# Keys as seven block products beside the values, sums of weight blocks in planes and in two stages

## The chip, the cores and the metric

The kernel runs on one core of a Trainium2 chip. The metric is the device time in microseconds of one execution; lower is better. The engines are TensorE (PE, its weight loads PEld), VectorE (DVE), ScalarE (ACT), GpSimd (POOL) and SyncE (SP), which issues nearly all DMAs.

## The reference

A trunk of two layers for 512 tokens of 2048 channels, in float32. What matters here is in the middle: after layer A, shared keys and values are projected from the residual stream, and layer B attends over them.

```python
kv = _rmsnorm(x, kv_norm) @ w_kv                      # 2048 x 4096: keys, then values
k = kv[..., :D_ATTN].reshape(bsz, s, N_HEADS, HEAD_DIM)   # 16 heads of 128
v = kv[..., D_ATTN:].reshape(bsz, s, N_HEADS, HEAD_DIM)
...
h = _rmsnorm(x, b_norm[lb])
proj = h @ b_w_in[lb]                                 # queries, then gates
o = _stick_breaking_attention(q, k, v)                # z = q k^T, sigmoids, a reverse running product, @ v
x = x + (o * jax.nn.silu(gate)) @ b_w_out[lb]
return _rmsnorm(x, final_norm)
```

## The kernel before, in words

Every float32 operand is split in two float32r parts, high and low, and a product is three matmuls: high by high, high by low, low by high (`product`, L730, whose matmul is at L733). ScalarE makes the high part of a staged weight tile (L1069 and L1071 with a gain for each row tile, L1067 without, L1209 and L1211 for the block products), VectorE the low part (L1538, L1540, L1535, L1748, L1751). A semaphore counts each step, and a tile of weights runs through a ring of four buffers: SyncE loads it when the low part of the tile four before is made, ScalarE splits it when TensorE has used the one four before.

There are five stages.

1. Layer A: 180 units of input projection and gates. A *unit* (`unit_t`, L737) is 256 rows by 256 columns of weights, weights still and all 512 tokens moving: 12 matmuls of 512 columns. Beside it, sums of 2 x 2 blocks of the value weights are made by VectorE (`block_sum`, L1685) from blocks that SyncE loads (`blocks_in`, L538) and stored to a scratch in HBM (`sums_out`, L548).
2. Output projection of layer A: 80 units. The new residual `x1` comes out in tiles of channels by tokens. GpSimd adds up token halves and channel pairs of it in `s_raw` (`token_sums`), the sums S1 to S4 of a Winograd form with seven products.
3. Values: `value_product` (L860). Seven block products p1 to p7 replace eight. VG = 2 groups of 1024 value columns, each of 7 x 8 = 56 products; a *block product* keeps 128 tokens still (twice) and moves 512 columns of weights: 6 matmuls of 512 columns. The operands come through six buffers (VRING), loaded in `operand_load` (L608). The results are drained and combined by ScalarE and VectorE into `v_f`, scaled by token and stored to a scratch (`v_store`, L598).
4. Layer B, in 8 pairs of heads: `pair_rest` (L959). N3 = 24 units each: 8 for queries, 8 for keys, 8 for gates (`src3`, L509). Its attention stands between units: scores of head 0 before unit 18, its transposes before unit 22, then, counted on into the next pair, scores of head 1 before unit 24 and so on to 30. `work3` (L1356 on ScalarE, L1918 on VectorE) gives the companions at the same positions. Queries are drained after unit 8 of a pair and keys after unit 16 (`kf`, L1929), both high parts are copied by ScalarE (L1361), both low parts subtracted by GpSimd (L2199), each in turn through the one tile `kf`. Sums of blocks of `b_w_out` are made beside it (`weight_sum`, `wb_load`, `wb_store`).
5. Output projection of layer B, again as block products (`out_product`), interleaved with the attention of the last pair, and the last norm.

VectorE's order within a pair is written out by hand in `body3` (L2051): the low part of unit q + 12, then a block sum if `W_SUM` names q, then `work3` for position q + 8. After the second head of a pair, that is `kf<-ps,sg` (L1884), three sums (L1899 to L1902), the next low part, two more sums (L1907, L1909). SyncE's order is written out in `weights3` (L661).

Of the kernel before, what the change touches and what calls it, by code (L numbers as in the profile page):

```python
# [27 lines left out]
F32 = mybir.dt.float32  # L28
# [5 lines left out]
P = 128  # L34
S = 512
# [20 lines left out]
N1, N2, N3 = 36, 20, 24  # L56
# [25 lines left out]
V_STORE, V_LOAD = 9, 18  # L82
# [10 lines left out]
VG, VP = 2, KD // 2  # L93
NO = 7 * VP
VOPS = VG * NO
VRING, AHEAD_V = 6, 5
# [11 lines left out]
T_IN, T_OUT = (16, 22, 34, 40), (27, 35, 45, 53)  # L108
T_SUM = {4: (0,), 5: (1,), 6: (2,), 7: (3,), 10: (4,), 11: (5,), 13: (6,), 16: (7, 8), 17: (9,)}
# [14 lines left out]

OPERAND = {operand(q): q for q in range(VOPS)}
OUT_LAST = 3


def out_operand(q):
# [9 lines left out]
    if g == VG - 1 and o >= 4 * VP:  # L139
        return g, (o - 4 * VP) % VP, ("p2", "p4", "p3")[(o - 4 * VP) // VP]  # L140
    return operand(q)


OUT_OPERAND = {out_operand(q): q for q in range(VOPS)}
OUT_RING = VOPS - VP
# [11 lines left out]
def build(nc, x, a_norm, a_w_in, a_conv_w, a_conv_b, a_w_r, a_b_r, a_w_i, a_b_i, a_lambda, a_w_out,  # L157
          kv_norm, w_kv, b_norm, b_w_in, b_w_out, final_norm, out):
    with ExitStack() as ctx:
# [56 lines left out]
        with ExitStack() as mem12:  # L216
# [13 lines left out]
            with ExitStack() as mem_v:  # L230
                v_f = sb("v_f", [P, TT, 1024], F32, mem_v)
# [3 lines left out]
                v_stage = sb("v_stage", [P, VRING - RING, 512], F32, mem_v)  # L235
        u2 = x1
        b_raw = b_raw0, b_raw1
        with ExitStack() as mem34:
# [11 lines left out]
            with ExitStack() as mem3:  # L250
                q_hi = sb("q_hi", [P, 2, S], F32R, mem3)
                q_lo = sb("q_lo", [P, 2, S], F32R, mem3)
# [74 lines left out]
        qk_f = sem("qk_f")  # L327
        qk_hi_ready = sem("qk_hi_ready")
        qk_lo_ready = sem("qk_lo_ready")
# [38 lines left out]
        wb_in = [sem(f"wb_in{n}") for n in range(2)]  # L368
# [31 lines left out]
        scaled_c = sem("scaled_c")  # L400
# [5 lines left out]
        def gain_column(phase, j):  # L406
# [3 lines left out]
            if phase == 3:  # L410
                return (C_GKV if j // 8 % 3 == 1 else C_GB) + 2 * (j % 8)
            return None

        def bank3(half, j):

            return 2 * ((3 * half + j // 8) % 2)
# [14 lines left out]
        def v_staged(q):  # L431

            slot = q % VRING
            return stage[:, slot, :] if slot < RING else v_stage[:, slot - RING, :]

        def v_weights(q):

            slot = q % VRING
# [3 lines left out]
        def kv_gain(k):  # L442

            return cT[:, C_GKV + k:C_GKV + k + 1]

# [33 lines left out]
        wt_scratch = nc.dram_tensor("wt_scratch", (4, VP * P, VG * 512), F32).ap()  # L479
        t_scratch = nc.dram_tensor("t_scratch", (4, VP * P, VG * 512), F32).ap()  # L480
# [6 lines left out]
        def _(sp):  # L487
# [1746 lines left out]
```

## Time and profile before

| | us |
|---|---|
| median of 3 runs (lowest, highest) | 1653.1 (1652.7, 1653.92) |
| profiled execution, whole | 1653.25 |
| its span in the profile | 1651.5 |
| TensorE busy | 1639.7 |
| VectorE busy | 1132.9 |
| ScalarE busy | 866.2 |
| GpSimd busy | 223.9 |
| mean DMA rate | 170 GB/s |

Busy times are sums over the span. Matmuls overlap their neighbours, so TensorE's busy share says that it is never idle for long, and not how fast it works: for that, the starts of successive matmuls are read. The stages in the trace: layer A to 506 us, its output projection to 731, the values to 887, the eight pairs to 1484, and the rest.

### The profile page before, as it was taken

What the parts mean: (1) busy time and instruction counts of PE and PEld (TensorE: products, weight loads), DVE (VectorE), ACT (ScalarE), POOL (GpSimd) and SP (SyncE); (2) the same over time, 40 slices, a digit from 0 to 9 for tenths busy, and PEclk for the clock granted to TensorE, in tenths of its full rate; (3) what the DMA queues carried; (4) which work ended last, traced back from release to release, by engine and by line L of the source; (5) the groups of instructions that cost most, each with busy time, mean ns of one, the idle gap of its engine ahead of it and who ended that gap; (6) DMA issues with size and microseconds to landing.
All of it is one profiled execution on the core that took longest, in us unless ns stands there. A gap on an engine that the chain in (4) does not pass through costs nothing.

```text
span 1651.5 us, 24337 instructions
## 1 busy us (share of the span) xinstructions
PE 1639.7 (99%) x7479; PEld 1364.7 (83%) x7479; DVE 1132.9 (69%) x1981; ACT 866.2 (52%) x1710; POOL 223.9 (14%) x221
## 2 busy tenths in 40 slices
PE   9999999999999999999999999999999999999997
PEld 8888888888888888888888888888888888888886
DVE  5788877778774545458654666666757576668867
ACT  7655566655565333346655544453545444446555
POOL 0121212121211313121000101110110101110000
PEclk9999999999999999999999999999999999999999
DMA  5556555655433343347675545445353636458875
GB/s 188 178 179 199 169 155 188 201 189 185 150 95 97 102 126 104 121 127 221 202 229 177 179 131 172 156 139 188 130 192 108 194 110 188 143 179 287 290 240 193
DMA packets 216839, 280.81 MB, mean 170 GB/s; under 512 B 16488, under 2 KB 145720, under 8 KB 216760
## 3 DMA queue, kind: packets, MB, share of 16 engines
q1 hardware_dynamic: 212152, 270.05, 51.4%
q10 hardware_dynamic: 4608, 9.83, 1.8%
q8 instruction: 34, 0.56, 0.1%
q14 instruction: 45, 0.37, 0.1%
HBM read 229.09 MB, written 50.72 MB: 169 GB/s over the span
## 4 chain that ended last, share of the span: by engine, by line
PE 96%; DVE 1%; ACT 1%; issue 0%; DMA 0%; POOL 0%; POOLq 0%; ACTq 0%; DVEq 0%
PE ps L733 94%; PE ps L943 1%; PE ps L763 0%; PE ps L833 0%; PE ps L789 0%; DVE oa_lo L1968 0%; DMA v_stage<-in_w_kv 0%; ACT rb L1460 0%; DVE x L2020 0%; ACT x L1506 0%; DVE rbuf L1677 0%; POOL y_lo L2133 0%; ACT w_hi L1067 0%; PE ps L770 0%; ACT abuf L1153 0%
## 5 line engine op out<-in xcount | busy, mean ns | idle before, releaser
L733 PE MATMUL ps<-x_hi,w_hi 128*128 128x512 f32 x1408 | 551.0, 391 | 0.1
L733 PE MATMUL ps<-x_hi,w_lo 128*128 128x512 f32 x1408 | 548.4, 389 | 0.0
L733 PE MATMUL ps<-x_lo,w_hi 128*128 128x512 f32 x1408 | 548.1, 389 | 0.0
L1538 DVE SCALAR_TENSOR_TENSOR w_lo<-stage,cT,w_hi 128x256 fp32r<-128x256 f32 x352 | 191.2, 543 | 285.1 <-ACT w_hi L1071 283.7
L1069 ACT ACTIVATE w_hi<-stage,cT 128x256 fp32r<-128x256 f32 x352 | 178.7, 508 | 374.7 <-PE ps L733 352.5
L733 PEld LDWEIGHTS ps<-x_hi,w_lo 128*128 128x128 f32 x1408 | 264.3, 188 | 55.0
L733 PEld LDWEIGHTS ps<-x_hi,w_hi 128*128 128x128 f32 x1408 | 264.5, 188 | 53.9 <-issue 0.7
L733 PEld LDWEIGHTS ps<-x_lo,w_hi 128*128 128x128 f32 x1408 | 264.5, 188 | 53.6 <-issue 0.2
L1071 ACT ACTIVATE w_hi<-stage,cT 128x256 fp32r<-128x256 f32 x352 | 174.4, 495 | 0.0
L1540 DVE SCALAR_TENSOR_TENSOR w_lo<-stage,cT,w_hi 128x256 fp32r<-128x256 f32 x352 | 172.4, 490 | 0.0
L1535 DVE TENSOR_TENSOR w_lo<-stage,w_hi 128x512 fp32r<-128x512 f32 x100 | 86.3, 864 | 116.5 <-ACT w_hi L1067 116.5
L1067 ACT ACTIVATE w_hi<-stage 128x512 fp32r<-128x512 f32 x100 | 62.6, 629 | 138.8 <-PE ps L733 138.1
L733 PE MATMUL ps<-y_hi,w_hi 128*128 128x512 f32 x320 | 125.3, 391 | 0.7 <-POOL y_lo L2133 0.7
L733 PE MATMUL ps<-y_hi,w_lo 128*128 128x512 f32 x320 | 124.6, 389 | 0.0
L733 PE MATMUL ps<-y_lo,w_hi 128*128 128x512 f32 x320 | 124.5, 389 | 0.0
L733 PEld LDWEIGHTS ps<-y_hi,w_hi 128*128 128x128 f32 x320 | 60.1, 188 | 13.2 <-POOL y_lo L2133 1.1
L733 PEld LDWEIGHTS ps<-y_hi,w_lo 128*128 128x128 f32 x320 | 60.1, 188 | 12.5
L733 PEld LDWEIGHTS ps<-y_lo,w_hi 128*128 128x128 f32 x320 | 60.1, 188 | 12.3
L1392 ACT ACTIVATE w_hi<-stage 128x512 fp32r<-128x512 f32 x70 | 43.8, 632 | 37.9 <-PE ps L733 34.7
L1968 DVE TENSOR_TENSOR w_lo<-stage,w_hi 128x512 fp32r<-128x512 f32 x70 | 47.5, 687 | 20.3 <-ACT w_hi L1392 20.0
L2206 POOL TENSOR_TENSOR wgt<-wgt,seen 128x128 f32<-128x128 f32 x64 | 35.2, 557 | 188.5 <-ACT wgt L1332 187.2
L2133 POOL TENSOR_TENSOR y_lo<-gate,y_hi 128x512 f32 x20 | 32.4, 1640 | 158.2 <-ACT y_hi L1165 158.2
(253 smaller groups left out, 2577.5 us busy)
## 6 DMA issues: line engine op xcount, KB each, us to landing
stage<-in_a_w_in SPq DMA_DIRECT2D x160, 256.0 KB, 2.8
stage<-in_b_w_in SPq DMA_DIRECT2D x128, 256.0 KB, 2.8
stage<-in_w_kv SPq DMA_DIRECT2D x95, 256.0 KB, 2.9
stage<-in_a_w_out SPq DMA_DIRECT2D x80, 256.0 KB, 2.6
b_raw<-in_w_kv SPq DMA_DIRECT2D x64, 256.0 KB, 4.1
t_scratch<-b_raw SPq DMA_DIRECT2D x64, 256.0 KB, 3.6
wb<-in_b_w_out SPq DMA_DIRECT2D x64, 256.0 KB, 4.8
wt_scratch<-wb SPq DMA_DIRECT2D x64, 256.0 KB, 3.3
```

Source lines behind the costliest of these rows:

```text
L733: mm = pe.matmul(dst, a, b, start=start and n == 0, stop=stop and n == 2, skip_group_check=not check)
L943: mm = pe.transpose(ps[bank][:, c + P * (i - k):c + P * (i - k) + P], wgt[:, W_OFF[i] + P * k:W_OFF[i] + P * k + P], ident[:, :])
L1067: nc.scalar.activation(w_hi[:, slot, :], stage[:, slot, :], ACT.Copy).then_inc(hi_ready, 1)
L1069: nc.scalar.activation(w_hi[:, slot, 0:256], stage[:, slot, 0:256], ACT.Identity, scale=cT[:, col:col + 1])
L1071: nc.scalar.activation(w_hi[:, slot, 256:512], stage[:, slot, 256:512], ACT.Identity, scale=cT[:, col + 1:col + 2]).then_inc(hi_ready, 1)
L1392: nc.scalar.activation(out_weights(q)[0], out_staged(q), ACT.Copy).then_inc(po_hi, 1)
L1535: nc.vector.tensor_tensor(w_lo[:, slot, :], stage[:, slot, :], f(w_hi[:, slot, :]), ALU.subtract).then_inc(lo_ready, 1)
L1538: nc.vector.scalar_tensor_tensor(w_lo[:, slot, 0:256], stage[:, slot, 0:256], cT[:, col:col + 1], f(w_hi[:, slot, 0:256]), ALU.mult, ALU.s ...
L1540: nc.vector.scalar_tensor_tensor(w_lo[:, slot, 256:512], stage[:, slot, 256:512], cT[:, col + 1:col + 2], f(w_hi[:, slot, 256:512]), ALU.m ...
L1968: nc.vector.tensor_tensor(lo_w, out_staged(q), f(hi_w), ALU.subtract).then_inc(po_lo, 1)
L2133: nc.gpsimd.tensor_tensor(y_lo[:, bass.ds(n * 2 + m, 1), :], gate[:, m:m + 1, :], f(y_hi[:, bass.ds(n * 2 + m, 1), :]), ALU.subtract).then ...
L2206: nc.gpsimd.tensor_tensor(diagonal, diagonal, seen[:, :], ALU.mult).then_inc(wgt_masked, 1)
```

## The change

- Keys leave the pairs. VG becomes 4: groups 2 and 3 of the block products are keys. Their products keep 128 columns of weights still (four times) and move 256 tokens of the inputs or token sums, so that results have channels as rows: 12 matmuls of 256 columns for a block product. The results are scaled by `rb` (the norm of each token, in columns) and go to a scratch `k_scratch`, from which SyncE loads the keys of a pair into `k_lo` (`k_load`).
- The pairs keep 16 units (N3 = 16): queries and gates. All positions of the attention move up by 8, and more of a pair's steps reach into the next one, and its store of results into the one after. Queries have a tile of their own (`q_f`, in the space of `q_lo`).
- The sums of key weight blocks are made in two stages: nine blocks (K_EARLY) during stage 2, in the unused half of `s_raw`, and seven during the first three groups of block products, in `kv_raw`.
- The scratches of block sums get one contiguous plane for each group.
- C11 of groups 2 and 3 is drained by VectorE (`take_k11`), the other key blocks are scaled by GpSimd. Stores of results are spread one by one over the next group.
- The ring of six buffers skips a slot twice. Loops over stage 2 on SyncE and VectorE are unrolled.

```diff
-N1, N2, N3 = 36, 20, 24
+N1, N2, N3 = 36, 20, 16
-V_STORE, V_LOAD = 9, 18
+K_LOAD, V_LOAD, O_STORE = 9, 16, 33
+LAST_STORE = {8: (0, 1), 10: (2, 3), 11: (4, 5), 13: (6, 7)}
-VG, VP = 2, KD // 2
+VG, VP = 4, KD // 2
+V_GROUPS = 2
+OG = 2
-W_SUM = {2: 0, 3: 1, 4: 2, 5: 3, 8: 4, 9: 5, 14: 6, 15: 7}
-W_IN, W_OUT = (14, 18), (22, 33)
+W_SUM = {0: (0, 1), 1: (2, 3), 12: (4, 5), 13: (6, 7)}
+W_IN, W_OUT = (12, 21), (18, 30)
+K_EARLY = VP + 1
...
+K_IN = {18 + 10 * n: 2 * n for n in range(4)} | {23 + 10 * n: 2 * n + 1 for n in range(4)} | {63: VP}
+K_OUT = {25 + 10 * n: 2 * n for n in range(4)} | {30 + 10 * n: 2 * n + 1 for n in range(4)} | {70: VP}
...
+K_FIRST, K_STEP = 32, 18
+KV_IN = {K_FIRST + K_STEP * n + VRING + 2 * e: (K_EARLY + n, e) for n in range(VP - 1) for e in range(4)}
+KV_OUT = {K_FIRST + K_STEP * n + VRING + 25 + 2 * e: (K_EARLY + n, e) for n in range(VP - 1) for e in range(4)}
+KV_SUM = {K_FIRST + K_STEP * n + at: (K_EARLY + n, e) for n in range(VP - 1) for e, at in enumerate((10, 12, 14, 17, 20))}
...
+RING_SKIPS = (3 * NO + 12, 3 * NO + 32)
+V_SLOT = [(q + sum(q >= skip for skip in RING_SKIPS)) % VRING for q in range(VOPS)]
...
-        t_scratch = nc.dram_tensor("t_scratch", (4, VP * P, VG * 512), F32).ap()
+        t_scratch = nc.dram_tensor("t_scratch", (4, VG, VP * P, 512), F32).ap()
+        k_scratch = nc.dram_tensor("k_scratch", (D, S), F32).ap()
...
             def src3(p, j):
-                w, half = ((b_w_in[0], 0), (w_kv, 0), (b_w_in[0], 1))[j // 8]
-                w = w.rearrange("r (n c) -> n r c", c=256)
-                return w[at(p + half * PAIRS, 1), 256 * (j % 8):256 * (j % 8) + 256, :].rearrange("n r c -> (n r) c")
+                w = b_w_in[0].rearrange("r (n c) -> n r c", c=256)
+                return w[at(p + (j // 8) * PAIRS, 1), 256 * (j % 8):256 * (j % 8) + 256, :].rearrange("n r c -> (n r) c")
...
+            def k_load(p):
+
+                if not isinstance(p, int) or p:
+                    sp.wait_ge(z_ready, p * 6)
+                src = k_scratch.rearrange("(n m p) c -> n p m c", m=2, p=P)[at(p, 1), :, :, :]
+                sp.dma_start(f(k_lo[:, :, :]), src.rearrange("n p m c -> (n p) m c")).then_inc(k_in, 16)
...
-            for q in range(VOPS):
-                if q == 4:
-                    sp.wait_ge(wb_out[0], 64 * VP)
+            for q in range(OOPS):
+                if q == 0:
+                    pair_event(V_LOAD, PAIRS - 1)
+                if q == 1:
+                    o_store(PAIRS - 2, 0)
+                if q == 2:
+                    pair_event(W_OUT[0], PAIRS - 1)
+                if q == 6:
+                    pair_event(W_IN[1], PAIRS - 1)
+                if q in range(43, 51, 2):
+                    wb_store(PAIRS - 1, 1, ((q - 43) // 2,))
                 out_load(q)
-                if q == 16:
-                    wb_store(PAIRS - 1, 1)
...
+                if g >= V_GROUPS:
+                    if name in V_SUM:
+                        which, banks = V_SUM[name]
+                        right = s_high(which, i), s_lo[:, which, i, :]
+                    else:
+                        m_hi, m_lo, odd, c, banks = V_LEFT[name]
+                        right = m_hi[:, 2 * i + odd, c:c + 256], m_lo[:, 2 * i + odd, c:c + 256]
+                    for t in range(2):
+                        for s in range(2):
+                            c = 256 * t + P * s
+                            mm = product(ps[banks[t]][:, 256 * s:256 * s + 256], hi_w[:, c:c + P], lo_w[:, c:c + P],
+                                         right[0], right[1], first_i and s == 0, i == VP - 1, check=False)
+                    mm.then_inc(op_used, 1)
+                    return
...
             def scores(it, half, h):
 
-                pe.wait_ge(qk_lo_ready, it * 8 + (4 * half + 4))
+                pe.wait_ge(k_lo_ready, it * 4 + (2 * half + 2))
+                pe.wait_ge(q_lo_ready, it * 4 + (2 * half + 2))
...
+                if g > V_GROUPS and o == AHEAD_V - 2:
+                    take_k11(g - 1)
...
+                if q in KV_SUM:
+                    key_sum(*KV_SUM[q])
...
+            def key_sum(m, n):
+
+                even, odd = kv_gain(2 * (m % VP)), kv_gain(2 * (m % VP) + 1)
+                b11, b12, b22, b21 = (key_block(m, e) for e in range(4))
+                if n == 0:
+                    dve.wait_ge(b_in[K_SET[m]], 64 * VP + 64 * (K_NTH[m] + 1))
+                    ins = nc.vector.tensor_tensor(b12, b11, b12, ALU.subtract)
+                elif n == 1:
+                    ins = nc.vector.tensor_scalar(b22, b22, odd, None, ALU.mult)
+                else:
+                    dve.wait_ge(t_made, 10 * VP + 5 * m + n)
+                    out, left, gain, op, right = ((b22, b12, even, ALU.add, b22), (b11, b11, even, ALU.subtract, b22),
+                                                  (b21, b21, odd, ALU.subtract, b22))[n - 2]
+                    ins = nc.vector.scalar_tensor_tensor(out, left, gain, right, ALU.mult, op)
+                ins.then_inc(t_made, 1)
+
+            def take_k11(g):
+
+                dve.wait_ge(op_used, OPERAND[g, VP - 1, "p2"] + 1)
+                dve.wait_ge(v_stored, 16 * 8 * g)
+                for t in range(2):
+                    nc.vector.tensor_tensor(by_half(v_f[:, t, 0:512]), by_half(ps[2 + t][:, :]), rb_of(0),
+                                            ALU.mult).then_inc(c11_taken, 1)
...
+            def take_query(p):
+
+                dve.wait_ge(w_used, p * N3 + (U3 + 8))
+                for m in range(2):
+                    nc.vector.tensor_tensor(q_f[:, m, :], ps[m][:, :], rb[:, :], ALU.mult).then_inc(q_taken, 1)
...
                     for q in range(N3):
-                        if q + LOOK == 15:
-
-                            work3(it, half, q + LOOK)
-                        if q + LOOK == 24:
+                        if q == N3 - 1 and not end:
+                            take_query(it * 2 + (half + 1))
+                        if q + LOOK == 16:
 
                             take_gate(it, half)
...
             def attention_parts(it, half):
 
                 p = it * 2 + half
-                for dst, src, c in ((q_lo, q_hi, 0), (k_lo, k_hi, 2)):
-                    for m in range(2):
-                        pool.wait_ge(qk_hi_ready, p * 4 + (c + m + 1))
-                        nc.gpsimd.tensor_tensor(dst[:, m, :], kf[:, m, :], f(src[:, m, :]),
-                                                ALU.subtract).then_inc(qk_lo_ready, 1)
+                for m in range(2):
+                    pool.wait_ge(k_hi_ready, p * 2 + (m + 1))
+                    nc.gpsimd.tensor_tensor(k_lo[:, m, :], f(k_lo[:, m, :]), f(k_hi[:, m, :]),
+                                            ALU.subtract).then_inc(k_lo_ready, 1)
+                for m in range(2):
+                    pool.wait_ge(q_hi_ready, p * 2 + (m + 1))
+                    nc.gpsimd.tensor_tensor(q_lo[:, m, :], q_f[:, m, :], f(q_hi[:, m, :]),
+                                            ALU.subtract).then_inc(q_lo_ready, 1)
```

## Rows read from the trace of the kernel before

**Rows 1.** The page: span, busy time of each engine, chain by engine

```profile
span 1651.5 us, 24337 instructions
...
PE 1639.7 (99%) x7479; PEld 1364.7 (83%) x7479; DVE 1132.9 (69%) x1981; ACT 866.2 (52%) x1710; POOL 223.9 (14%) x221
...
PE 96%; DVE 1%; ACT 1%; issue 0%; DMA 0%; POOL 0%; POOLq 0%; ACTq 0%; DVEq 0%
```

**Rows 2.** Waits, whole span: who waited for whom, us, times, longest

```profile
PE ps L733 <- POOL y_lo L2133: 0.7, 1, 0.7
...
PEld ps L733 <- issue: 2.9, 10, 0.7
```

**Rows 3.** The chain in order of time: start, us, engine and line, count

```profile
43.78 465.18 PE ps L733 x2052
...
1046.47 52.84 PE ps L733 x240
...
1121.70 52.84 PE ps L733 x240
```

**Rows 4.** Timeline of TensorE, end of one head's scores: start, us, instruction

```profile
1012.49 0.27 PE L733 MATMUL ps<-k_hi,q_lo 128*128 128x128 f32 x1
1012.60 0.34 PE L733 MATMUL ps<-k_hi,q_hi 128*128 128x256 f32 x1
1012.77 0.28 PE L733 MATMUL ps<-k_lo,q_hi 128*128 128x256 f32 x1
1012.89 0.28 PE L733 MATMUL ps<-k_hi,q_lo 128*128 128x256 f32 x1
1013.01 0.39 PE L733 MATMUL ps<-x_hi,w_hi 128*128 128x512 f32 x1
```

**Rows 5.** Timeline of TensorE, in one head's values

```profile
1039.06 0.29 PE L733 MATMUL ps<-wt_hi,v_hi 128*128 128x256 f32 x1
1039.19 0.28 PE L733 MATMUL ps<-wt_lo,v_hi 128*128 128x256 f32 x1
1039.30 0.29 PE L733 MATMUL ps<-wt_hi,v_lo 128*128 128x256 f32 x1
1039.43 0.22 PE L733 MATMUL ps<-wt_hi,v_hi 128*128 128x128 f32 x1
```

**Rows 6.** Groups by shape, 740 to 886 us; then the tile b_raw, with its transfers

```profile
L1748 DVE SCALAR_TENSOR_TENSOR w_lo<-stage,cT,w_hi 128x512 fp32r<-128x512 f32 x39 | 30.8, 795 | 21.1 <-ACT w_hi L1209 21.1
...
L1209 ACT ACTIVATE w_hi<-stage,cT 128x512 fp32r<-128x512 f32 x39 | 28.1, 722 | 24.0 <-PE ps L733 20.0 <-DMA stage<-t_scratch 4.0
...
L1699 DVE SCALAR_TENSOR_TENSOR b_raw<-b_raw,cT x48: 737/747/1797, 60.3 to 436.5; 128x512 f32<-128x512 f32 x48
...
DMA to landing us min/median/max: 2.3/3.9/6.9
```

**Rows 7.** Stretches: length, PE, PEld, DVE, ACT, POOL busy, granted clock, DMA share, GB/s

```profile
743.00:786.00 43.00, 43.00 (x191) 35.46 (x190) 37.34 (x64) 28.46 (x56) 5.23 (x5) 1.00 0.71 222
...
900.00:1484.00 584.00, 584.00 (x2760) 491.17 (x2759) 381.76 (x726) 276.47 (x621) 72.68 (x92) 1.00 0.50 159
1524.00:1544.00 20.00, 20.00 (x89) 16.28 (x88) 18.34 (x29) 13.69 (x24) 0.00 (x0) 1.00 0.94 334
```

**Rows 8.** Timeline of all engines, from one pair's end to the next scores

```profile
1056.62 0.51 ACT L1069 ACTIVATE w_hi<-stage,cT 128x256 fp32r<-128x256 f32 x1 [3.73 <-PE ps L733]
...
1059.99 0.42 DVE L1902 TENSOR_TENSOR ost<-kf 128x256 f32<-128x256 f32 x1
...
1063.86 1.28 DVE L1929 TENSOR_TENSOR kf<-ps,rb 128x512 f32<-128x512 f32 x2
...
1065.28 2.54 POOL L2199 TENSOR_TENSOR q_lo<-kf,q_hi 128x512 fp32r<-128x512 f32 x2 [27.57 <-ACT q_hi L1361]
...
1081.10 1.29 DVE L1929 TENSOR_TENSOR kf<-ps,rb 128x512 f32<-128x512 f32 x2 [0.89 <-PE ps L733]
...
1086.34 0.39 PE L733 MATMUL ps<-k_hi,q_hi 128*128 128x512 f32 x1
```

More of the change, by code:

```diff
@@ L586, in load2, with key_block_in @@
                 load(a_w_out[0, rows:rows + 256, at(it * 512 + 256 * (j // 10))], j, False, it * N2 + (U2 + j))
-            for j in range(N2):
-                load2(0, j)
-            with sp.Fori(1, B2) as it:
+            def key_block_in(m, n):
+                if n == 0:
+                    sp.wait_ge(t_out[K_SET[m]], 64 * VP + 64 * K_NTH[m])
+                g, i = divmod(m, VP)
+                odd, half = ((0, 0), (0, 1), (1, 1), (1, 0))[n]
+                row, col = P * (2 * i + odd), 1024 * g + 512 * half
+                sp.dma_start(key_block(m, n), w_kv[row:row + P, col:col + 512]).then_inc(b_in[K_SET[m]], 16)
@@ L591, in _, with key_sum_out @@
+            def key_sum_out(m, e):
+                if e == 0:
+                    sp.wait_ge(t_made, 10 * VP + 5 * m + 5)
+                n, which = ((1, T1), (2, T2), (0, T3), (3, T4))[e]
+                g, i = divmod(m, VP)
+                sp.dma_start(t_scratch[which][V_GROUPS + g][P * i:P * i + P, :],
+                             key_block(m, n)).then_inc(t_out[K_SET[m]], 16)
+            for it in range(B2):
                 for j in range(N2):
                     load2(it, j)
-                    if j in (3, 13):
+                    if it and j in (3, 13):
@@ L1483, in body3 @@
                                 out_step(n)
-                        if q + LOOK != 15 and not (end and q == N3 - 1):
+                        if q == N3 - 3 and not end:
+                            key_hi(it * 2 + (half + 1))
+                        if not (end and q == N3 - 1):
                             work3(it, half, q + LOOK)
@@ L1834, in body2 @@
                         work2(it, q + LOOK)
+                    if N2 * it + q in K_SUM:
+                        m, sums = K_SUM[N2 * it + q]
+                        for n in sums:
+                            key_sum(m, n)
                     if last and q == LOOK + 4:
@@ L1839, in body2 @@
                         value_step(6)
-            with dve.Fori(0, B2 - 1) as it:
+            for it in range(B2 - 1):
                 body2(it, False)
@@ L2069, in body3 @@
                                 out_step(n)
-                        if q in W_SUM:
-                            weight_sum(it, half, W_SUM[q])
-                        if q + LOOK != 15 and not (end and q == N3 - 1):
+                        for n in W_SUM.get(q, ()):
+                            weight_sum(it, half, n)
+                        if not (end and q == N3 - 1):
                             work3(it, half, q + LOOK)
@@ L2173, in _ @@
             squares(VP - 1)
+            pool.wait_ge(rb_ready, 2)
+            for g in range(V_GROUPS, VG):
+                for ready, rows, h in ((c22_ready, (2, 3), 1), (c21_ready, (2, 3), 0), (c12_ready, (0, 1), 1)):
+                    for n, t in enumerate(rows):
+                        pool.wait_ge(ready, 2 * g + n + 1)
+                        one = by_half(v_f[:, t, 512 * h:512 * h + 512])
+                        nc.gpsimd.tensor_tensor(one, one, rb_of(t // 2), ALU.mult).then_inc(k_scaled, 1)
             pool.wait_ge(op_used, VOPS)
```

351 lines of the change are left out of this document (205 added, 146 removed).

## The prediction

> **What bounds the kernel now.** I read the busy times first. TensorE's matmuls cover 1639.7 of 1651.5 us, and the granted clock is 1.00 in the stretches that I looked at, its upper level of 2.4 GHz [rows 1, 7]. Matmuls are pipelined, so this alone could hide gaps. The chain that ended last says the same in another way: 96% of it is TensorE [rows 1]. The waits leave nothing to doubt: the product helper waits 0.7 us in all, once, on GpSimd [rows 2]. So the time is the sum of start-to-start distances on TensorE, and any change is read as: how many matmuls go, how many come, how far apart they start, and whether a new wait opens.
>
> The duration of a matmul of 512 columns, 0.39 us [rows 4], isn't that distance, for neighbours overlap. In the chain, 2052 matmuls, all of 512 columns, take 465.18 us [rows 3]: **0.2267 us for each**. (The 240 that take 52.84 us hold twelve shorter ones of the scores, hence their mean of 0.220.)
>
> **What goes.** Each of 8 pairs loses 8 units of key projection, with 2 channel tiles, 2 row tiles and 3 products each: 12 matmuls. 8 x 8 x 12 = 768, and 768 x 0.2267 = 174.1 us of a chain without holes.
>
> **What comes.** Two groups of 56 block products. A key product sets the weights still and moves 256 columns of the inputs: 2 x 2 x 3 = 12 matmuls of 256 columns with 12 weight loads. 2 x 56 x 12 = 1344. In columns this is 344,064 for 393,216, seven eighths; in instructions it is 1.75 times as many, so all hangs on the distance at 256 columns. The kernel has such matmuls in short runs only. In the scores they follow matmuls of 128 columns: starts at 1012.60, 1012.77, 1012.89, and the next matmul at 1013.01: 0.17, 0.12, 0.12 [rows 4]. In the values they follow 384 columns and are followed by 128: 0.13, 0.11, 0.13 [rows 5]. The lower bound is half of the 512 case, 0.1134. The upper one is the mean of the scores' three, 0.41 / 3 = 0.137. The change makes runs of hundreds, which are nearest to the second and third of a row: I take 0.118, between 0.11 and 0.12. 1344 x 0.118 = 158.6 us. At the bounds it is 152.4 and 184.1; with the values' mean, 0.37 / 3 = 0.123, it is 165.8. Net: 174.1 - 158.6 = **15.5 us less**, from 21.7 less to 10.0 more.
>
> Why 256 isn't simply half: two neighbours of 128 columns start 0.11 apart (1012.49 and 1012.60 [rows 4]), about half of 0.2267, where a quarter, 0.057, would be their share. Something of 0.11 us is paid for each matmul whatever its width, and with one weight load to each matmul the load is the candidate. At 256 columns it is just covered: 0.11 under 0.1134. There is nothing left to hide anything else in.
>
> The Trainium skill, "TensorE: Matmul & The Clock Gate", section "Part 3: Packing small matmuls — row/col tiling", has a rule against the change: a weight load overlaps running matmuls only where the row groups differ. All of these use the whole array, so load and columns would add up, 0.11 + 0.1134 = 0.223 us, and 1344 of them 300 us, 126 us more than what goes. The trace disagrees: full loads stand before full matmuls and the distance is 0.12 [rows 4].
>
> **What else is moved, on the other engines.** In the order of the kernel:
>
> - *Nine key blocks summed in the output-projection stage of layer A.* Each costs VectorE five operations; the block sums of today have three of 0.75 us each [rows 6] among theirs, and with as much for the other two I get 3.7 us. 9 x 3.7 = 33 us in a stage of some 220 us on an engine that TensorE's splits fill by less than half there (0.8 us in 2.72). Transfers: 9 x 2 MB. Nobody but later reads waits. Cost 0. Two of GpSimd's token sums wait for stores that were issued tens of steps before. Cost 0.
> - *The value stage becomes 224 products.* ScalarE's split is 0.72 us and VectorE's 0.79 [rows 6] for every 12 x 0.118 = 1.42 us of TensorE. VectorE over 18 products (25 us): 18 x 0.79 = 14.2, a key block 3.7, drains 10 x 0.64 for 56 products, 2.1: 20 of 25, 80%. The first third of today's stage has it at 37.34 of 43 us, 87%, with no product delayed [rows 7]. Six buffers let it lag some 5 us. Cost 0.
> - *SyncE's queue and the transfers.* For 18 products: 18 loads, 4 key loads, 4 key stores of 256 KB, and 8 result stores for 56 products: 28.6 x 0.262 MB in 25 us is 300 GB/s, for 190 us. One stretch of today's kernel moves 334 GB/s at a share of 0.94, with TensorE at 20.00 of 20 [rows 7]. So it fits, at 0.85, though never for so long. VectorE's first operation on a key block waits for the last of its four loads, issued 4 steps (5.6 us) ahead; the like landed in 3.9 us, 6.9 at worst [rows 6]. Behind that wait stand VectorE's splits, and TensorE behind them, with the 5 us of lag as cover. I take 0.5 us for the whole stage, 0 to 10 as bounds.
> - *The drain of C11 between the third and fourth group goes to VectorE*, after its split: 0.72 + 0.79 + 2 x 0.64 (a drain, [rows 8]) = 2.8 us and the signals between, while TensorE has 2 products, 2.84 us. Cost 0.3 us, once; bounds 0 and 1. (After the second group it stays on ScalarE, without VectorE's split before it.)
> - *The attention stage shrinks from 24 to 16 units a pair.* A pair is now 1121.70 - 1046.47 = 75.2 us [rows 3], and 75.2 - 8 x 2.72 = 53.4 after. VectorE: 381.76 of 584 us [rows 7], so 49.2 a pair; it loses 8 splits of at least 0.79 [rows 6] and two drains of 0.64: 41.6 of 53.4, 78%. ScalarE has more room. Transfers: 159 GB/s x 75.2 = 12.0 MB; 2 MB of weights go, 0.5 MB of keys come: 10.5 MB in 53.4 us, 197 GB/s. Cost 0. Keys are loaded four units (11 us) ahead of their split.
> - *The query's chain* has no such room. Queries are now the last to be ready before the scores. Their drain stands behind the previous pair's last sums on VectorE. In the trace these end at 1059.99 + 0.42 = 1060.41 [rows 8], while the drain could start at 1056.6 + 2.72 = 1059.3 (ScalarE's split at 1056.62 marks the unit before). From the drain's start to the end of GpSimd's two subtractions: 1065.28 + 2.54 - 1063.86 = 3.96 us [rows 8]. 1060.41 + 3.96 = 1064.37. The scores start 1086.34 - 1081.10 = 5.24 us after the drain could start [rows 8]: 1059.3 + 5.24 = 1064.5. Slack 0.15 us, where the keys' chain, which starts at 1081.10 without delay, has 5.24 - 3.96 = 1.3. I take 0.1 us of waiting for each of 8 pairs, 0.8 in all; bounds 0 and 1 us each.
> - *The start of the output stage* gets 1 MB of weight blocks, 1 MB of their sums and half a MB of values that were moved earlier before; they come ahead of the stretch at 334 GB/s [rows 7], and products don't wait there now. The four stores of the last sums go from product 16 to products 43 to 49, behind that stretch. Cost 0, bounds 0 and 2. *Two skipped slots in the ring* leave five buffers instead of six for a few products, 4 x 1.42 us of cover instead of 5. *Contiguous planes* change addresses alone. Cost 0.
> - *Edge of a longer straight run of TensorE code with twice the instructions per us*: the nearest row is that of the weight loads, which waited for "issue" 10 times and 2.9 us in all [rows 2], hidden by 512 columns. Bounds 0 and 3 us; I take 0.4.
>
> **The sum.** The profiled execution took 1653.25 us, 1651.5 of it span [rows 1]. 1653.25 - 15.5 + 0.5 + 0.3 + 0.8 + 0.4 = 1639.75. The median of the runs is 0.15 below the profiled one: **1639.6 us**.
>
> **Rivals.**
>
> *A. The weight load shows.* If a key matmul costs what the scores' three cost on average, 0.137 us, 184.1 us come for 174.1: 1653.1 + 10.0 + 2.0 = 1665, slower. For it: the first of the three stands 0.17 off, and each weight is used once. Against it: the other five distances are 0.11 to 0.13, and the 0.17 follows a backlog of 128-column matmuls. It decides from 174.1 / 1344 = 0.1295 us. Chance 0.09.
>
> *B. The query's chain is late* by 1 us in each pair: 1639.6 + 8 x 0.9 = 1647. For it: the slack of 0.15 us. Against: GpSimd and ScalarE are otherwise free there. Chance 0.13.
>
> *C. Transfers or VectorE fall behind in the value stage*: seven late key blocks at 1.5 us of waiting each on TensorE, 10 us: 1650. For it: 300 GB/s for 190 us. Against: 334 GB/s without a delayed product [rows 7]. Chance 0.15, of which 0.04 within 0.2% and 0.02 slower.
>
> *D. Load and columns add up*, as that rule has it: 1653 + 126 = 1779. Against it the distances of [rows 4, 5]. Chance 0.01.
>
> **How the numbers follow.** The forecast itself has 0.62, and with A to D that is 1. Its own ends are 0.1134 with no waits, 1631, and 0.123 with the small costs, 1647. The range goes from 1631 to 1651, to take in B and most of C; A and D stay outside. 0.2% is 3.3 us, about what a measurement of this kernel can tell from no change. Faster: 0.62 + 0.13 + 0.09 = 0.84. Within: 0.04 from C and 0.01 from A, 0.05. Slower: 0.08 + 0.02 + 0.01 = 0.11.
>
> **What would show it.** In the profile after: 7479 - 768 + 1344 = 8055 matmuls; a run of key products in which starts stand 0.118 us apart (0.1295 or more is A); pairs 53.4 us apart; waits of TensorE on GpSimd's q_lo of about 0.1 us eight times (B: near 1); no waits on v_wlo or w_lo above 1 us in the value stage (C: several). The prediction is wrong if the distance at 256 columns in a long run isn't what it is in runs of three.

## The result, and the profile after

The changed kernel takes **1642.9 us** (median of 4 runs, 1642.3 to 1643.95) where the kernel before, beside it on the same chip, takes 1653.5 (1652.7 to 1654.1): a ratio of 0.9934, interval 0.9922 to 0.9947. The profiled execution took 1642.97 us with a span of 1641.2, 10.3 us less than the span of [rows 1]. It is faster, inside the range, 3.3 us above the forecast of 1639.6. The forecast of the gain was 13.5 us; it is 10.6 here and 12.2 in a second measurement (the run control).

Page of the changed kernel, busy time by engine:

```profile
PE 1626.5 (99%) x8055; PEld 1380.8 (84%) x8055; DVE 1226.7 (75%) x2053; ACT 886.7 (54%) x1698; POOL 250.9 (15%) x233
```

8055 matmuls, as counted ahead. TensorE is still 94% of the chain, now with one unbroken piece of 1440 matmuls: 384 of 512 columns in the value groups and 1056 of 256 in the key groups, up to the last product p5 of the last group. The VectorE row after it is the drain that the next row's products wait for (start, length, what):

```profile
43.76 465.18 PE ps L836 x2052
...
799.60 213.91 PE ps L836 x1440
1016.81 1.21 DVE v_f L1907 x2
1018.06 70.54 PE ps L836 x432
...
1111.01 31.07 PE ps L836 x144
1143.18 20.20 PE ps L836 x96
1164.47 31.08 PE ps L836 x144
...
1507.01 5.64 DMA stage<-wt_scratch
1514.05 8.51 DMA stage<-in_b_w_out
1524.94 1.28 issue
```

The first row is the one of [rows 3] to the digit: 512 columns still cost 0.2267 us. A pair lasts 1164.47 - 1111.01 = 53.46 us (75.2 before, 53.4 forecast). The last three rows are new: before, the chain had no transfer in this place.

Timeline of TensorE among the key products of the changed kernel (start, duration, instruction):

```profile
899.72 0.28 PE L836 MATMUL ps<-s_hi,w_lo 128*128 128x256 f32 x1
899.84 0.28 PE L836 MATMUL ps<-s_hi,w_hi 128*128 128x256 f32 x1
899.96 0.28 PE L836 MATMUL ps<-s_lo,w_hi 128*128 128x256 f32 x1
900.08 0.28 PE L836 MATMUL ps<-s_hi,w_lo 128*128 128x256 f32 x1
```

Starts are **0.120 us** apart; 1330 of the 1343 distances in the two key groups are that, to the nanosecond. In stretches (length, then PE, PEld, DVE, ACT and POOL busy, granted clock, share of the transfer engines, GB/s), three of the value stage and one of the output stage:

```profile
829.00:859.00 30.00, 30.00 (x134) 24.86 (x133) 21.74 (x34) 15.97 (x24) 0.00 (x0) 1.00 0.94 323
...
889.00:919.00 30.00, 30.00 (x252) 30.00 (x251) 21.07 (x32) 17.37 (x28) 0.00 (x0) 1.00 0.96 334
919.00:949.00 30.00, 30.00 (x252) 30.00 (x251) 22.55 (x31) 14.32 (x22) 3.00 (x2) 1.00 0.82 259
...
1511.00:1531.00 20.00, 17.99 (x79) 14.35 (x78) 17.11 (x26) 12.61 (x23) 0.00 (x0) 1.00 0.95 326
```

In these stretches of the value stage nothing is late, at a share of up to 0.96. In the output stage TensorE loses 2 us of 20, at a share and a rate like those of the stretch of before in [rows 7], where it lost none.

Put together, by three points of the two traces. The first is the matmul that spreads the norms of the tokens; it stands 68 us into the value stage, ahead of all the matmuls that the change adds or takes. Up to it: -0.4 us (799.4 and 799.0). From it to the first output product: 684.3 us before and 672.2 after, **-12.1**. The output stage: 167.8 and 170.0, **+2.2**. That is -10.3.

### The profile page after: what moved, and what is told of

Same layout as the page of the kernel before. It is cut to its first block, busy times and chain, and to the rows that moved or that the text cites. A ratio compares the mean times of both kernels' runs of the same rounds, so it can differ in the third digit from the quotient of the medians.

```text
span 1641.2 us, 25385 instructions
## 1 busy us (share of the span) xinstructions
PE 1626.5 (99%) x8055; PEld 1380.8 (84%) x8055; DVE 1226.7 (75%) x2053; ACT 886.7 (54%) x1698; POOL 250.9 (15%) x233
## 4 chain that ended last, share of the span: by engine, by line
PE 94%; DVE 2%; DMA 1%; ACT 1%; issue 1%; POOL 0%; SPq 0%; DVEq 0%; POOLq 0%; ACTq 0%
PE ps L836 92%; PE ps L1062 1%; DMA stage<-in_b_w_out 1%; PE ps L936 0%; DMA stage<-wt_scratch 0%; PE ps L866 0%; DMA xraw<-in_x 0%; ACT rb L1584 0%; DVE w_lo L2123 0%; DVE x L2175 0%; DVE rbuf L1802 0%; POOL y_lo L2287 0%; DVE x_lo L1699 0%; DVE oa_lo L2123 0%; ACT w_hi L1186 0%
## 5 line engine op out<-in xcount | busy, mean ns | idle before, releaser
L836 PE MATMUL ps<-x_hi,w_hi 128*128 128x512 f32 (+1 forms) x1276 | 486.8, 382 | 0.5 <-DVE x_lo L1699 0.3
L836 PE MATMUL ps<-x_hi,w_lo 128*128 128x512 f32 (+1 forms) x1276 | 483.8, 379 | 0.0
L836 PE MATMUL ps<-x_lo,w_hi 128*128 128x512 f32 (+1 forms) x1276 | 483.7, 379 | 0.0
L1188 ACT ACTIVATE w_hi<-stage,cT 128x256 fp32r<-128x256 f32 x288 | 146.0, 507 | 283.5 <-PE ps L836 263.2
L1663 DVE SCALAR_TENSOR_TENSOR w_lo<-stage,cT,w_hi 128x256 fp32r<-128x256 f32 x288 | 158.4, 550 | 168.9 <-ACT w_hi L1190 168.2
L836 PEld LDWEIGHTS ps<-x_hi,w_lo 128*128 128x128 f32 x1276 | 240.0, 188 | 45.1
L836 PEld LDWEIGHTS ps<-x_hi,w_hi 128*128 128x128 f32 x1276 | 240.2, 188 | 44.6 <-issue 0.8
L836 PEld LDWEIGHTS ps<-x_lo,w_hi 128*128 128x128 f32 x1276 | 240.2, 188 | 43.6 <-issue 0.2
L1665 DVE SCALAR_TENSOR_TENSOR w_lo<-stage,cT,w_hi 128x256 fp32r<-128x256 f32 x288 | 144.1, 500 | 0.0
L1190 ACT ACTIVATE w_hi<-stage,cT 128x256 fp32r<-128x256 f32 x288 | 142.8, 496 | 0.0
L1873 DVE SCALAR_TENSOR_TENSOR w_lo<-stage,cT,w_hi 128x512 fp32r<-128x512 f32 x87 | 68.4, 788 | 42.4 <-ACT w_hi L1328 41.8
L1328 ACT ACTIVATE w_hi<-stage,cT 128x512 fp32r<-128x512 f32 x87 | 62.8, 722 | 55.6 <-PE ps L836 54.2
L836 PEld LDWEIGHTS ps<-y_lo,w_hi 128*128 128x128 f32 x320 | 60.1, 188 | 12.2
```

The lines of the kernel that those rows point to most:

```text
L836: mm = pe.matmul(dst, a, b, start=start and n == 0, stop=stop and n == 2, skip_group_check=not check)
L1188: nc.scalar.activation(w_hi[:, slot, 0:256], stage[:, slot, 0:256], ACT.Identity, scale=cT[:, col:col + 1])
L1190: nc.scalar.activation(w_hi[:, slot, 256:512], stage[:, slot, 256:512], ACT.Identity, scale=cT[:, col + 1:col + 2]).then_inc(hi_ready, 1)
L1328: ins = nc.scalar.activation(dst, v_staged(q), ACT.Identity, scale=kv_gain(2 * i + odd))
L1663: nc.vector.scalar_tensor_tensor(w_lo[:, slot, 0:256], stage[:, slot, 0:256], cT[:, col:col + 1], f(w_hi[:, slot, 0:256]), ALU.mult, ALU.s ...
L1665: nc.vector.scalar_tensor_tensor(w_lo[:, slot, 256:512], stage[:, slot, 256:512], cT[:, col + 1:col + 2], f(w_hi[:, slot, 256:512]), ALU.m ...
```

## Experiments

The runs were measured on several chips, each with the kernel before beside it, which took 1653.5 to 1654.0 us in the median.

### The same kernel again, and the stores of the last sums (control, late_stores, early_stores, early_spread)

The stalls of the output stage lie at 1522 and 1524 us, near the place where the change puts the stores of the last sums. The edit of late_stores:

```diff
-                if q in range(43, 51, 2):
-                    wb_store(PAIRS - 1, 1, ((q - 43) // 2,))
+                if q in range(59, 67, 2):
+                    wb_store(PAIRS - 1, 1, ((q - 59) // 2,))
```

early_stores has all four at `q == 24`, early_spread one each at 24, 26, 28 and 30; control has no edit.

> The changed kernel once more, as the control for the other runs. Every theory: a ratio of 0.993 to 0.994 to the kernel before (1642.9 us for 1653.5). The question is the output stage, which was 2.3 us longer than before in the profile (two stalls of TensorE at 1522.2 and 1524.5, 1.1 and 1.7 us). If the stalls come from the order in which loads and stores stand, they are there again, at the same products and of like size; if they are an accident of one execution, they move or vanish.

> The changed kernel with one edit: the four stores of the last sums of weight blocks stand at output products 59, 61, 63, 65 in SyncE's queue instead of 43 to 49. Theory S (the stores there compete with the loads, which the prediction had excluded): the two stalls go, the output stage is 167.7 us again and the time some 2.3 us under the changed kernel's. Rival T (the backlog comes from what the stage loads in the 15 us before, and the stores are bystanders, for the first of them was issued after the latencies had begun to climb): the stalls stay within 0.5 us of 2.3 in all and the time stays within 1 us.

> The changed kernel with one edit: all four stores of the last sums stand at output product 24 (near product 16, where they stood in the kernel before) instead of 43 to 49. Theory S: the stores then lie ahead of the dense stretch and the stalls go, -2.3 us. Rival T: no change, or a backlog that begins earlier (1 MB more in front of the dense stretch), +0 to +3 us.

> The changed kernel with the four stores of the last sums at output products 24, 26, 28 and 30, one at a time, instead of 43 to 49. So far the stall in the output stage near product 44 to 46 was 2.3, 0.5, 1.0 us (stores from 43 on, also in the control), 1.0 (stores from 59 on) and 0.07 us (all four at 24). Theory E (stores ahead of the dense stretch space out the loads behind them, and that removes most of the stall): stall under 0.4 us, stage 167.7 to 168.0 us, 1641.0 to 1641.4 us. Rival F (the size of the stall is chance from one execution to the next, whatever the stores do): anything from 0 to 2.3 us, 1641.5 or more in the median.

Measured: control 1641.7 us (ratio 0.9925, interval 0.9910 to 0.9941), late_stores 1642.2, early_stores 1641.1, early_spread 1644.2 (0.9942, 0.9928 to 0.9955). Waits in the output stage (us in total, times, longest), control and then early_spread:

```profile
PEld ps L836 <- issue: 1.0, 1, 1.0
...
PE ps L836 <- issue: 0.6, 1, 0.6
```

```profile
PEld ps L836 <- issue: 3.7, 2, 2.2
...
PE ps L836 <- issue: 2.9, 2, 1.8
```

late_stores still stalls, by 1.2 us, with no store of those sums anywhere near: the stall doesn't need the stores at product 43 to 49. The trace of the changed kernel agrees. The load behind its first stall was issued at 1514.05 and took 8.51 us (above), and the first of the stores was issued at 1522.41, when that load was all but landed. early_stores fitted theory E, and early_spread, made to confirm it, is the worst of all. It was measured on another chip than early_stores and the control, though, and all five of its times (1644.1 to 1645.5) lie above all of theirs, so the order and the chip are not separated here. Every traced kernel of the study gives a sample of this stage, for most of them don't touch it. Its length, from the first output product to the end of the span:

| kernel | stores of the last sums | stage, us |
|---|---|---|
| before / planes_only / before_8k | at 16, as before | 167.8 / 167.8 / 168.5 |
| changed / control / strided / pitch_10k | at 43 to 49 | 170.0 / 168.2 / 168.9 / 170.3 |
| key_widths / extra_traffic / query_late / key_512 | at 43 to 49 | 169.3 / 169.3 / 168.5 / 167.8 |
| late_stores / early_stores / early_spread | 59 / 24 / 24 to 30 | 169.1 / 167.7 / 171.1 |

The stall comes in the same place, products 44 to 46, and its size changes from one traced execution to another, down to nothing; it is there in one of three executions with the order of before too. The eight executions with the change's order average 169.0 us, the three with the old one 168.0. So about 1 us may belong to the order and about 1 us to the execution or the chip that was profiled; eleven samples with this spread don't prove the first. No edit here makes a version that is shown to be better: early_stores is 0.6 us under the control, with overlapping ranges of runs (1640.6 to 1641.9, and 1641.6 to 1641.7).

### What sets 0.120 us (key_512, key_widths)

key_512 gives the key groups the form of the value groups; in key_widths the slices of the moving operand are 192 columns wide in the first key group and 320 in the second.

```diff
-                if g >= V_GROUPS:
+                if g >= VG:
```

```diff
-                        right = m_hi[:, 2 * i + odd, c:c + 256], m_lo[:, 2 * i + odd, c:c + 256]
+                        right = tuple(x[:, 2 * i + odd, c:c + (192, 320)[g - V_GROUPS]] for x in (m_hi, m_lo))
```

> The changed kernel with one edit: the two key groups of the value stage take the form of the value groups, 6 matmuls of 512 columns to a block product instead of 12 of 256, with the same loads, splits and drains. It leaves the keys in the wrong layout, and so leaves out that part of what the change does. Theory W (256 columns cost 0.120 us, and 512 cost 0.2267, because a weight load to each matmul is 0.12 us and the columns of 256 are just under it): 112 products go from 12 x 0.120 = 1.44 to 6 x 0.2267 = 1.36 us, 9 us less than the changed kernel (ratio to before near 0.988), and the weight loads are busy for some 83% of the key stretches or less, instead of all of them. Rival (the 0.120 is half of the 512 case and some fixed gap at a change of operands, splits or signals): under 3 us of difference.

> The changed kernel with other widths of the key products' matmuls, everything else as it is: in the first key group (672 matmuls) 192 columns are moved, in the second (672) 320, in place of 256. It leaves out or repeats part of the keys' columns, and its keys are wrong. Theory W (a distance has a floor of about 0.12 us for the weight load, and above it goes by the columns): 192 columns stay at 0.11 to 0.12 us, 320 are at 0.142 to 0.147. Rival L (no floor at these widths: by the line through 256 at 0.120 and 512 at 0.2267 us, 0.0133 us plus 0.000417 for each column): 192 columns 0.093, 320 columns 0.147. In time: W some +16 to +18 us to the changed kernel less 0 to 5, so 1654 to 1660; L 0 us, 1642.

key_512 took 1633.8 us, 7.9 under the control, and the part from the value stage to the first scores 268.1 us for 276.6: 8.5 of the 9 expected. Its weight loads cover 24.86 of 30 us, as in all stretches of 512 columns:

```profile
910.00:940.00 30.00, 30.00 (x134) 24.86 (x133) 24.31 (x36) 15.73 (x24) 2.99 (x2) 1.00 0.90 313
```

key_widths took 1655.7 (one execution). Timeline of TensorE, first group and second:

```profile
905.04 0.27 PE L836 MATMUL ps<-x_hi,v_wlo 128*128 128x192 f32 x1
905.15 0.28 PE L836 MATMUL ps<-x_hi,v_whi 128*128 128x192 f32 x1
905.26 0.27 PE L836 MATMUL ps<-x_lo,v_whi 128*128 128x192 f32 x1
...
1002.85 0.31 PE L836 MATMUL ps<-x_hi,v_wlo 128*128 128x320 f32 x1
1003.00 0.31 PE L836 MATMUL ps<-x_hi,v_whi 128*128 128x320 f32 x1
1003.14 0.31 PE L836 MATMUL ps<-x_lo,v_whi 128*128 128x320 f32 x1
```

The means of some 670 distances each are 0.1116 us at 192 columns and 0.1467 at 320. Theory W holds, with one correction that matters for the forecast. 320, 256 and 512 columns lie on one line, 0.1467, 0.120 and 0.2267: 0.0133 us and 0.000417 for each column. 192 columns would be at 0.0933 on it and are at 0.1116, held up by the floor. So 256 columns are *above* the floor and cost their columns and the fixed part; the floor isn't what makes them 0.120. The weight loads, busy in 30.00 of 30 us, look as if they were the limit, and they aren't: a narrower matmul still starts sooner. What makes the floor stays open. The weight load is the candidate, but every matmul in these traces has one, so no run separates it from another cost of each matmul.

The line was to be had from the kernel before. Its timeline in one head's values, just ahead of [rows 5]:

```profile
1038.54 0.33 PE L733 MATMUL ps<-wt_hi,v_hi 128*128 128x384 f32 x1
1038.71 0.34 PE L733 MATMUL ps<-wt_lo,v_hi 128*128 128x384 f32 x1
1038.88 0.34 PE L733 MATMUL ps<-wt_hi,v_lo 128*128 128x384 f32 x1
```

0.52 us from 1038.54 to the matmul at 1039.06 are 0.173 for 384 columns. Through 512 at 0.2267 that gives 0.00042 us for each column and 0.119 to 0.120 at 256.

### The planes (planes_only, strided, pitch_10k, before_8k)

planes_only is the kernel before with the sums in planes; strided the changed kernel without them. Of both arrays in strided, here the shape and one address:

```diff
-        t_scratch = nc.dram_tensor("t_scratch", (4, VG, VP * P, 512), F32).ap()
+        t_scratch = nc.dram_tensor("t_scratch", (4, VP * P, VG * 512), F32).ap()
-                sp.dma_start(t_scratch[which][V_GROUPS + g][P * i:P * i + P, :],
+                sp.dma_start(t_scratch[which][P * i:P * i + P, 512 * (V_GROUPS + g):512 * (V_GROUPS + g) + 512],
```

pitch_10k changes `VG * 512` to `VG * 512 + 512` in strided; before_8k changes it to `2 * VG * 512` in the kernel before.

> The kernel before with one part of the change alone: the sums of weight blocks of both projections are kept in contiguous planes (one for each column group) instead of side by side in rows twice as long. Theory P0 (the prediction's step: addresses alone, cost 0): the time is that of the kernel before within 1 us, the output stage stays 167.7 us, and its loads in the dense stretch land in 5.3 to 6.8 us as before. Rival P1 (contiguous 256 KB blocks are served more slowly, or collide more, and that is what made the changed kernel's output stage 2.3 us longer): the same loads land in 7 us or more and the output stage is 0.5 to 2.5 us longer. Rival P2: contiguous planes are a gain of 1 to 3 us.

> The changed kernel with that part undone: sums side by side in rows twice as long, as in the kernel before. P0: the time of the control (1641.7 us) within 1 us, stalls in the output stage of 0.5 to 2.5 us in all as in the three runs so far with the stores at 43 or later (2.3, 0.8 and 1.4 us). P1: no stalls there, 1640 to 1641 us. P2: 1 to 3 us slower than the control.

> The run strided (sums of blocks side by side in rows of 8 KB, 2048 numbers) with one edit: rows of 10 KB (2560 numbers, the last 512 unused), so that the pieces of 2 KB of one block stand 10 KB apart instead of 8. In strided, the stores of those sums in layer A took 6.24 us to land on average (4.31 in the changed kernel, 4.32 in the kernel before with rows of 4 KB), and layer A was 10 us longer. Theory M (it is the step of 8 KB, which brings the pieces of a block to few places of the memory): the stores land in 4.2 to 4.8 us and the time is within 2 us of the control's 1641.7. Rival N (it is that blocks are not contiguous at all over so large an array): the stores stay above 5.5 us and the time is 1650 or more.

> The kernel before with one edit: its sums of value weights stand in rows of 8 KB (the second half unused) instead of 4 KB. Theory M: the step of 8 KB alone brings the loss: the stores land in about 6.2 us, layer A is some 10 us longer, 1662 to 1665 us. Rival M2 (in the run strided it took something else of the changed kernel as well, its larger amount of scratch memory or other places of its buffers): the stores stay near 4.3 us and the time near 1654.

planes_only: 1654.1 us, ratio 0.9998 (0.9989 to 1.0007), 11 runs. strided: **1653.3 us**, ratio 0.9994 (0.9985 to 1.0003), 11 runs, so all of the gain is lost. None of the three theories on record for strided foresaw that. The loss is in layer A, hundreds of us ahead of the products that the change is about: the matmul that spreads the norms comes at 810.2 us for 799.5 in the control, and from there to the output stage both take 672.2. The stretch 60 to 500 us of the changed kernel, and then of strided:

```profile
60.00:500.00 440.00, 440.00 (x1943) 364.34 (x1942) 350.99 (x600) 264.83 (x494) 82.63 (x54) 1.00 0.54 171
```

```profile
60.00:500.00 440.00, 434.95 (x1897) 354.44 (x1896) 343.71 (x591) 258.35 (x487) 77.77 (x52) 1.00 0.62 169
```

TensorE starts 46 matmuls fewer in strided, 10.4 us at 0.2267 each. The transfer engines are busier (0.62 for 0.54) while they move a little less. Transfers of 220 to 420 us, with KB each and the median to landing: changed kernel, strided, pitch_10k and before_8k, the stores of the sums in each, and in the first two the weight loads of layer A:

```profile
stage<-in_a_w_in SPq DMA_DIRECT2D x65, 256.0 KB, 2.7
t_scratch<-b_raw SPq DMA_DIRECT2D x36, 256.0 KB, 3.4
```

```profile
stage<-in_a_w_in SPq DMA_DIRECT2D x63, 256.0 KB, 3.0
t_scratch<-b_raw SPq DMA_DIRECT2D x32, 256.0 KB, 6.3
```

```profile
t_scratch<-b_raw SPq DMA_DIRECT2D x36, 256.0 KB, 3.4
```

```profile
t_scratch<-b_raw SPq DMA_DIRECT2D x32, 256.0 KB, 6.0
```

A block's 128 pieces of 2 KB, written 8 KB apart, take 6.0 to 6.3 us; written 4 KB apart (before), 10 KB apart or side by side they take 3.4 to 3.5. The weight loads behind them are late. Waits in the stretch 60 to 500 us (us in total, times, longest), changed kernel and then strided:

```profile
ACT w_hi L1188 <- DMA stage<-in_a_w_in: 18.5, 7, 2.8
```

```profile
ACT w_hi L1188 <- DMA stage<-in_a_w_in: 43.0, 8, 6.4
...
PEld ps L836 <- DVE w_lo L1665: 12.3, 18, 0.9
...
PE ps L836 <- DVE w_lo L1665: 5.0, 15, 0.5
```

ScalarE waits for the loads, and in strided TensorE then for the splits, for which it doesn't wait in the changed kernel. pitch_10k, one execution, took 1644.1 us, with all 440.00 us of the stretch covered and its excess over the control in the output stage (170.3 us). before_8k, one execution, took 1663.9 us, 10.3 over the kernel before and above all nine times of it (1653.1 to 1657.6). The step of 8 KB alone is the cause, and needs nothing else of the change; nor is it the size of the array, which is larger still in pitch_10k. What in the memory makes it so wasn't tested.

### The room of the transfers (extra_traffic)

```diff
+                if m >= K_EARLY:
+                    sp.dma_start(extra[4 * (m - K_EARLY) + n], w_kv[row:row + P, col:col + 512]).then_inc(extra_in, 16)
```

> The changed kernel with 28 more transfers of 256 KB, from memory to memory, one beside each block load of the seven late key blocks in the value stage (7.3 MB, some 40 MB/ms more where the stage already moves 259 to 334 GB/s in stretches of 30 us). Theory R (the transfers of the value stage have room left, which is why rival C of the prediction did not come): waits for loads under 2 us in all, time within 2 us of the control. Rival C2 (the stage is at the edge, .96 of the transfer engines in one stretch): products wait, 3 to 15 us more.

1644.0 us, 2.3 over the control. Of that, 1.1 is the output stage (169.3 for 168.2); from the value stage to the first scores there are 277.4 us for 276.6, so 28 more transfers cost 0.8 us. Two stretches of 30 us in it, the second with a delay of 0.5 us that the changed kernel doesn't have:

```profile
829.00:859.00 30.00, 30.00 (x134) 24.82 (x134) 19.86 (x31) 15.38 (x24) 0.00 (x0) 1.00 0.99 349
859.00:889.00 30.00, 29.54 (x131) 24.13 (x130) 20.22 (x32) 16.20 (x24) 0.00 (x0) 1.00 0.98 357
```

The chain ahead of that delay, in order of time:

```profile
851.49 5.99 DMA stage<-in_w_kv
...
857.50 0.74 ACT w_hi L1333
...
858.93 1.29 DVE v_f L1912 x2
...
860.26 1.89 PE ps L841 x7
```

The delayed product doesn't wait for its own weights. A late load delays a split on ScalarE, that delays the split on VectorE, and VectorE's drain of C22, which stands behind it, is what TensorE waits for. Most of the lateness is hidden: in the whole stage VectorE waits 9.0 us for block loads (0.9 in the changed kernel). Theory R holds for the time and for TensorE, not for its "under 2 us" if that is read as all engines' waits. In this one execution 349 GB/s cost TensorE nothing and 357 cost 0.5 us; the change moves at most 334 there. That is no rule for the rate alone, for the output stage stalls at 326.

### The query's chain (query_late)

```diff
-                dve.wait_ge(w_used, p * N3 + (U3 + 8))
+                dve.wait_ge(w_used, p * N3 + (U3 + 9))
```

> The changed kernel with one edit: the drain of the queries waits for one more projection unit of TensorE, though it doesn't need it. In the changed kernel GpSimd's last q_lo ends 0.30 to 0.34 us before the scores start in seven pairs (1.28 in the first), and the drain starts 4.2 to 4.3 us before the scores, some 1.0 us after it could. One unit is 2.72 us. Theory Q (the chain has 0.3 us of slack, the prediction's 0.15 being an estimate of the same; beyond it TensorE waits one for one): the drain comes 1.7 us later, TensorE waits 1.4 us in each pair, 11.5 us in all, about 1654 us. Rival Q2 (the chain isn't on the path because the scores wait for something else, or the drain is late for another reason): under 4 us.

1655.2 us (one execution), 13.5 over the control; 13.2 of it lie between the matmul that spreads the norms and the output stage. Timeline of the changed kernel and, after it, of query_late, GpSimd's last subtraction and the first matmul of the scores:

```profile
1127.51 1.29 POOL L2371 TENSOR_TENSOR q_lo<-q_f,q_hi 128x512 fp32r<-128x512 f32 x1
...
1129.11 0.39 PE L836 MATMUL ps<-k_hi,q_hi 128*128 128x512 f32 x1
```

```profile
1131.33 1.27 POOL L2371 TENSOR_TENSOR q_lo<-q_f,q_hi 128x512 fp32r<-128x512 f32 x1
...
1132.74 0.47 PE L836 MATMUL ps<-k_hi,q_hi 128*128 128x512 f32 x1 [1.41 <-POOL q_lo L2371]
```

Where TensorE does wait, it starts 0.14 us after the subtraction's end, in all eight pairs; that is the time from the signal to the start. In the changed kernel the distance is 1129.11 - 1128.80 = 0.31, so its real slack is **0.17 us**. Pairs last 55.13 us for 53.47: the drain comes 1.85 us later, less the slack is 1.68, and 1.66 are measured. Theory Q holds; my 1.4 came of counting 0.3 as slack.

## Why the prediction came out as it did

- **What goes**, 174.1 us at 0.2267 each: right; 512 columns cost the same before and after.
- **What comes**, 158.6 us at 0.118: the term that was mis-sized. 1344 x 0.120 = 161.3, 2.7 us more. The prediction chose between 0.11 and 0.12, printed values of a hundredth, and took half of the 512 case, 0.1134, for the lower bound. It can't be: 0.0133 us of the 0.2267 are fixed and don't halve. Two widths above the floor give a line and with it the missing width. "Just covered" was right: the floor is 0.11 and the distance 0.120.
- **Value stage**: 0.5 us for transfers and 0.3 for C11's drain. No product waited for a transfer; one waited for a drain, that of C22 ahead of the first product p3 of the last group (its start and the next come 0.4 us late in all), not that of C11. The wait was put on the wrong tile, and that its size came near is chance. Rival C, 10 us, is out: the waits from the added products on come to some 0.7 us. Its path is real, and extra_traffic shows it at work.
- **The query's chain**: a slack of 0.15 us forecast, 0.17 found, and the agreement is luck. The forecast is the gap between GpSimd's end and the scores; that gap is 0.30 to 0.34 us in seven pairs, because the drain starts 0.97 us after it could and not 1.11. The forecast left out the 0.14 us of the signal, and the two misses cancel. The 3.96 us from the drain's start to the subtractions' end came out to the digit. The step after it failed: with a positive slack that repeats to 0.04 us in seven pairs there is nothing to charge, and the 0.8 us on top were a hedge, not a reading. Rival B fell for the same reason.
- **Edge of straight-line code**, 0.4 us: half of it at most. Weight loads wait 0.5 us for "issue" in the value stage, matmuls not at all; two distances of the key products are 0.22 and 0.21 us instead of 0.120, 0.2 us in all.
- Together these make -12.1 for -13.5 us up to the output stage: 2.7 more for the products, and 1.3 of the 2.0 us of small waits not needed. The 0.4 us ahead of the first point are not the change's: the control is 0.1 us later there than the kernel before.
- **The output stage** at cost 0, bounds 0 and 2: the profiled execution lost 2.2, the control 0.4. This stage holds the difference between the two measurements of the gain: of the 1.6 us, 0.4 is the kernel before (1653.5 and 1653.9) and 1.2 the changed one, whose two traces differ by 1.8 us here and by 0.5 us the other way before it. The stated reason, stores "behind that stretch", was wrong in place (the first is issued at 51 us of the stage, inside the dense part), yet the runs show that the stall doesn't need these stores. The step that failed is the one before: that at 334 GB/s "products don't wait there now" was read from one execution of before, as a property of the kernel. The same stage lasts 167.8 to 170.3 us in eight traces with one order. Why one execution stalls and another doesn't stays open.
- **Planes** at cost 0, since they "change addresses alone": right for the edit by itself, wrong as a statement on this change. With four column groups side by side the rows become 8 KB, and without the planes the change would have been worth nothing. The prediction compared with the rows of before; it had to compare with what the rest of the change would have made of them.
- **Rivals A and D** fell with 0.120 against 0.1295 and 0.223. On D the Trainium skill, "TensorE: Matmul & The Clock Gate", says in "Part 3: Packing small matmuls — row/col tiling", in the list of what overlaps, that a weight load overlaps running matmuls only where row groups differ; 1344 full-array matmuls at 0.120 us, each with its load, show that here it does overlap.

## What to carry to other kernels

Where a change alters the width of many matmuls, fit a line through two widths that the trace has and look for the floor separately, from the narrowest; here a width above the floor cost its columns plus the fixed part. When an array in memory grows, work out the distance of its rows before and after: a step of 8 KB between pieces of 2 KB cost as much as this whole change gained, in a stage that has nothing to do with it. A stage in which the transfer engines are 0.94 busy needs several traces, on more than one chip, before "nothing waits there" is taken from it. And where an added wait is priced from a gap, take the time of the signal off the gap first: 0.14 of 0.31 us here.

## What the hardware showed that I had not expected

- Stores of 128 pieces of 2 KB: 3.4 to 3.5 us (median to landing) at steps of 2, 4 and 10 KB, 6.0 to 6.3 at 8 KB.
- Start-to-start of matmuls with a weight load each: 0.1116 us at 192 columns, 0.120 at 256, 0.1467 at 320, 0.2267 at 512. The weight loads read as busy all the time at 256 columns, and still don't set the distance.
- With the same order of loads and stores, a stage that moves some 330 GB/s over 20 us lasted 167.8 to 170.3 us in eight traces.
